# Input projection of a two-block layer: three rolled loops written out, fewer column sums of squares, and a gate product with its weight halves side by side

## The reference, cut to what matters

```
h = rmsnorm(x, norm1_w);  proj = h @ w_in            # 1024 x 3592
q,k,v (3 x 4 heads x 128) = silu(causal_dwconv(proj[:, :1536], conv_qkv_w))
z (4 x 128), b_a (4), a_a (4), then 3 x 512 columns for a second attention
qa = l2norm(qa) * 128**-0.5;  ka = l2norm(ka)        # v is not normalized
beta = sigmoid(b_a);  g = -exp(a_log) * softplus(a_a + dt_bias)
```

## Time and profile before

| | |
|---|---|
| runs, median (lowest to highest) | 2656.86 us (2655.59 to 2659.09) |
| the profiled execution | 2655.63 us |
| its span, first to last instruction | 2654.0 us |
| mean granted TensorE clock | 0.985 |
| busy: PE, PEld, VectorE, ScalarE, GpSimd | 96%, 78%, 57%, 40%, 3% |

### The profile page before, as it was taken

One profiled execution on the slowest core, in us unless ns is written; L12 is line 12 of the kernel. 1 busy time (PEld: TensorE's weight loads), 2 busy tenths in 40 slices (PEclk: granted clock), 3 DMA queues, 4 the chain that ended last, 5 costly groups with the idle time before them and its releaser, 6 DMA issues.

```text
span 2654.0 us, 36131 instructions
## 1 busy us (share of the span) xinstructions
PE 2536.4 (96%) x14218; PEld 2078.6 (78%) x14218; DVE 1506.7 (57%) x2521; ACT 1061.4 (40%) x1715; POOL 67.2 (3%) x118
## 2 busy tenths in 40 slices
PE   6999988999989999999999999979999999999997
PEld 4878866777768788888788888868888788888886
DVE  4114325656536666665648964476588755655555
ACT  3123323544534534444544454443334433423332
POOL 1000000000000000000000000000000000000000
PEclk9999998999999999999999999999999999999999
DMA  5322212111034455556444555522333333333331
GB/s 187 96 80 89 86 67 95 45 36 55 2 119 129 153 184 198 197 197 204 152 134 128 168 173 175 159 72 82 93 88 88 89 107 90 103 114 100 96 96 64
DMA packets 318470, 304.35 MB, mean 115 GB/s; under 512 B 10223, under 2 KB 277860, under 8 KB 318180
## 3 DMA queue, kind: packets, MB, share of 16 engines
q1 hardware_dynamic: 303332, 243.92, 31.4%
q0 software_dynamic: 14976, 58.20, 5.4%
HBM read 244.41 MB, written 57.67 MB: 114 GB/s over the span
## 4 chain that ended last, share of the span: by engine, by line
PE 84%; DVE 8%; ACT 3%; issue 3%; DMA 2%; SPq 0%; POOLq 0%; POOL 0%; DVEq 0%; ACTq 0%
PE PS L2020 13%; PE PS L2021 13%; PE PS L2022 13%; PE PS L1726 11%; PE PS L2037 6%; PE PS L2039 6%; PE PS L2038 6%; PE PS L1967 3%; PE PS L1851 3%; PE PS L1979 1%; PE PS L1837 1%; PE PS L1955 1%; DVE wl L1276 1%; DVE cg L1673 1%; ACT wh L939 1%
## 5 line engine op out<-in xcount | busy, mean ns | idle before, releaser
L2020 PE MATMUL PS<-hh,wh 128*128 128x512 f32 x1728 | 682.7, 395 | 4.3 <-DVE wl L1276 1.9
L2022 PE MATMUL PS<-hh,wl 128*128 128x512 f32 x1728 | 672.9, 389 | 0.0
L2021 PE MATMUL PS<-hl,wh 128*128 128x512 f32 x1728 | 672.5, 389 | 0.0
L939 ACT ACTIVATE wh<-raw 128x1024 fp32r<-128x1024 f32 x352 | 366.7, 1055 | 514.2 <-PE PS L2039 381.1
L1276 DVE TENSOR_TENSOR wl<-raw,wh 128x1024 fp32r<-128x1024 f32 x286 | 347.8, 1227 | 390.2 <-ACT wh L939 389.9
L1569 DVE TENSOR_TENSOR x<-x,PS 128x512 f32<-128x512 f32 x432 | 293.8, 685 | 180.9 <-PE PS L2039 180.1
L2020 PEld LDWEIGHTS PS<-hh,wh 128*128 128x128 f32 x1728 | 324.5, 188 | 76.8 <-issue 5.0
L2021 PEld LDWEIGHTS PS<-hl,wh 128*128 128x128 f32 x1728 | 324.5, 188 | 70.6 <-issue 4.6
L2022 PEld LDWEIGHTS PS<-hh,wl 128*128 128x128 f32 x1728 | 324.3, 188 | 67.8
L2037 PE MATMUL PS<-fh,wh 128*128 128x512 f32 x864 | 344.2, 398 | 18.7 <-DVE x L1569 10.9
L2038 PE MATMUL PS<-fl,wh 128*128 128x512 f32 x864 | 339.4, 393 | 0.0
(11 more groups left out here) (292 smaller groups left out, 2547.8 us busy)
## 6 DMA issues: line engine op xcount, KB each, us to landing
raw<-in_w_ff SPq DMA_DIRECT2D x128, 512.0 KB, 4.0
raw<-in_w_up SPq DMA_DIRECT2D x88, 512.0 KB, 4.4
wl_s<-wl POOLq DMA_DIRECT2D x66, 512.0 KB, 5.4
wl<-wl_s SPq DMA_DIRECT2D x66, 512.0 KB, 3.6
raw<-in_w_in SPq DMA_DIRECT2D x60, 512.0 KB, 4.0
raw<-in_w_down SPq DMA_DIRECT2D x44, 512.0 KB, 5.1
raw<-in_w_out SPq DMA_DIRECT2D x32, 512.0 KB, 3.9
qkvz_s<-st POOLq DMA_DIRECT2D x16, 512.0 KB, 2.9
```

Of the source, the lines that this page charges most:

```text
L939: A(whs(slot), raw[:, k % 2], ACT.Copy).then_inc(s["w_hi"], 1)
L2020: mm(bank, wh[:, k % 4, cut], hh[:, kk, span(a_)], start=kk == 0, stop=False)
L2021: mm(bank, wh[:, k % 4, cut], hl[:, kk, span(a_)], start=False, stop=False)
L2022: last = mm(bank, wl[:, k % 4, cut], hh[:, kk, span(a_)], start=False, stop=kk == KT - 1)
```

## The change

- The five rolled loops over units 12 to 23 are written out, so that each unit can differ.
- The column sums of squares are made for `4*i + u` from 1 to 8 alone, that is for the eight units of q and k. The first square, its semaphore `sq_init` and TensorE's wait for it go. The units of v have no square: their Silu raises `st_written` itself.
- The high and low gate weights lie side by side in one tile `bahl` of 16 columns. One product with `hh` gives high x high and low x high in partitions 0 to 7 and 8 to 15, one with `hl` gives high x low (and low x low, which was not made before). Two products in place of three; the transposes are 16 rows high, and VectorE adds the two halves after them (two more instructions).
- ScalarE waits for `st_written` to reach 24 ahead of the gate copy, and for `st_written` ahead of `cacc` in the last two units of v, in place of the waits that the squares gave.

```diff
-        bah, bal, baw = sb("bah", [P, 8, 8], F32R), sb("bal", [P, 8, 8], F32R), sb("baw", [P, 8, 8])
+        bahl, baw = sb("bahl", [P, 8, 16], F32R), sb("baw", [P, 8, 8])
+        bah, bal = bahl[:, :, 0:8], bahl[:, :, 8:16]
...
# the rolled loops of SyncE, GpSimd's queue, ScalarE, VectorE and TensorE, each:
-            with sp.Fori(0, 3) as i:
+            for i in range(3):
...
# ScalarE
-            act.wait_ge(s["st_written"], 12)
-            A(sqb[:], st[:, 3], ACT.Square).then_inc(s["sq_init"], 1)
...
+                    if i == 2 and u >= 2:
+                        act.wait_ge(s["st_written"], 11 + 4 * i + u)
                     A(cacc[:, u % 2], acc(u % 2), ACT.Copy,
                       scale=par[:, bass.ds(C_CONV + 36 + 4 * i + u, 1)]).then_inc(s["tap0"], 1)
                     act.wait_ge(s["conv"], 12 * i + 3 * u + 3)
                     act.wait_ge(st_free[u], 48 + 16 * i)
-                    A(st[:, u], cacc[:, u % 2], ACT.Silu).then_inc(s["silu"], 1)
-                    act.wait_ge(s["silu"], 4 * i + u + 1)
-
-                    act.wait_ge(s["col_mm"], 4 * i + u + 1)
-                    A(sqb[:], st[:, u], ACT.Square).then_inc(s["st_written"], 1)
+                    if i < 2:
+                        A(st[:, u], cacc[:, u % 2], ACT.Silu).then_inc(s["silu"], 1)
+                        act.wait_ge(s["silu"], 4 * i + u + 1)
+                        if i or u:
+                            act.wait_ge(s["col_mm"], 4 * i + u)
+                        A(sqb[:], st[:, u], ACT.Square).then_inc(s["st_written"], 1)
+                    else:
+                        A(st[:, u], cacc[:, u % 2], ACT.Silu).then_inc(s["st_written"], 1)
             act.wait_ge(s["ba_mm"], 1)
-            A(cacc[0:8, 1, :], acc(2)[0:8], ACT.Copy).then_inc(s["ba_copied"], 1)
+            act.wait_ge(s["st_written"], U_Z)
+            A(cacc[0:16, 1, :], acc(2)[0:16], ACT.Copy).then_inc(s["ba_copied"], 1)
...
# VectorE
-            dve.wait_ge(s["silu"], 12)
-            dve.wait_ge(s["col_mm"], 12)
+            dve.wait_ge(s["st_written"], U_Z)
+            dve.wait_ge(s["col_mm"], 8)
...
-            ba = PS[:, 6, 0:64].rearrange("p (t c) -> p t c", c=8)
+            both = PS[:, 6, 0:128].rearrange("p (t c) -> p t c", c=16)
+            ba = tmpt[:, 7].rearrange("p (t c) -> p t c", c=8)
+            done(V_.tensor_copy(tmpt[:, 6].rearrange("p (t c) -> p t c", c=8), both[:, :, 8:16]))
+            done(TTo(ba, both[:, :, 0:8], tmpt[:, 6].rearrange("p (t c) -> p t c", c=8), ALU.add))
...
# TensorE
-            pe.wait_ge(s["sq_init"], 1)
...
-                    pe.wait_ge(s["st_written"], 12 + 4 * i + u)
-                    for tt in range(TT):
-                        last = mm(PS[:, 7, bass.ds(tt * 12 + 4 * i + u, 1)], sqb[:, tt * P:(tt + 1) * P], ones[:, 0:1],
-                                  start=True, stop=True)
-                    last.then_inc(s["col_mm"], 1)
+                    if 0 < 4 * i + u <= 8:
+                        pe.wait_ge(s["st_written"], 12 + 4 * i + u)
+                        for tt in range(TT):
+                            last = mm(PS[:, 7, bass.ds(tt * 12 + 4 * i + u, 1)], sqb[:, tt * P:(tt + 1) * P], ones[:, 0:1],
+                                      start=True, stop=True)
+                        last.then_inc(s["col_mm"], 1)
...
             for kk in range(KT):
-                for n, (w, h) in enumerate(((bah, hh), (bah, hl), (bal, hh))):
+                for n, h in enumerate((hh, hl)):
                     for q in range(2):
-                        last = mm(PS[0:8, 4 + q, :], w[:, kk, :], h[:, kk, q * HALF:(q + 1) * HALF],
-                                  start=kk == 0 and n == 0, stop=kk == KT - 1 and n == 2)
+                        last = mm(PS[0:16, 4 + q, :], bahl[:, kk, :], h[:, kk, q * HALF:(q + 1) * HALF],
+                                  start=kk == 0 and n == 0, stop=kk == KT - 1 and n == 1)
...
-                        last = tr(PS[:, 6, 8 * t:8 * t + 8], cacc[0:8, 1, t * P:(t + 1) * P], ident[0:8, 0:8])
+                        last = tr(PS[:, 6, 16 * t:16 * t + 16], cacc[0:16, 1, t * P:(t + 1) * P], ident[0:16, 0:16])
```

More of the change, by code:

```diff
@@ L697, in program @@
         names = """const_loaded rows_loaded pack_loaded par_mm par_ready consts_set xt_mm x_written x_spilled w_hi w_lo
-            w_used n_sq n_v n_sd n_diag n_R n_x n_hi n_lo n_lo_odd v_chain tap0 conv silu sq_init
+            w_used n_sq n_v n_sd n_diag n_R n_x n_hi n_lo n_lo_odd v_chain tap0 conv silu
             col_mm ba_loaded ba_hi ba_lo ba_mm ba_copied st_written phase_end tab_dve tab_act tab_mm tables_loaded
@@ L891, in _ @@
                 pool.dma_start(qkvb_s[:, n], st[:, n % 4]).then_inc(st_free[n % 4], 16)
-            with pool.Fori(0, 3) as i:
+            for i in range(3):
                 for u in range(4):
@@ L974, in _ @@
             act.wait_ge(s["ba_loaded"], 16)
-            A(bah[:], baw[:], ACT.Copy).then_inc(s["ba_hi"], 1)
+            A(bah, baw[:], ACT.Copy).then_inc(s["ba_hi"], 1)
             for n in range(12):
@@ L983, in _ @@
                 A(st[:, n % 4], acc(n % 2), ACT.Copy, scale=(0.125 if n < 4 else 1.0)).then_inc(s["st_written"], 1)
-            act.wait_ge(s["st_written"], 12)
-            A(sqb[:], st[:, 3], ACT.Square).then_inc(s["sq_init"], 1)
-            with act.Fori(0, 3) as i:
+            for i in range(3):
                 for u in range(4):
@@ L1343, in _ @@
             dve.wait_ge(s["ba_hi"], 1)
-            TTo(bal[:], baw[:], bah[:].bitcast(F32), ALU.subtract).then_inc(s["ba_lo"], 1)
+            TTo(bal, baw[:], bah.bitcast(F32), ALU.subtract).then_inc(s["ba_lo"], 1)
             for n in range(12):
                 prep(n + 2, (n + 2) % 4)
-            with dve.Fori(0, 3) as i:
+            for i in range(3):
                 for u in range(4):
@@ L1795, in _ @@
                 unit(n, n % 4, n % 2, stats=0 if n == 0 else None)
-            pe.wait_ge(s["sq_init"], 1)
-            with pe.Fori(0, 3) as i:
+            for i in range(3):
                 for u in range(4):
```

## The result

The changed kernel took 2638.14 us (median of 4 runs, 2636.18 to 2639.78) against 2656.23 us for the kernel before beside it; the ratio is 0.9931, 95% interval 0.9914 to 0.9948. It is faster by about 18 us, where 15.2 were forecast, and the median lies 3.6 us under the forecast of 2641.7 us. That is outside the forecast's own range (2639.5 to 2643.5 us) and 0.14 us inside the wide one (2638 to 2646.5 us). The profiled execution took 2636.18 us, with a span of 2634.4 us.

A forecast was written before the change was run, and what follows sets the result against it. TensorE, whose matmuls hold 84% of the span, was taken as the bound. 4.26 + 7.25 + 3.70 = 15.2 us off the 2656.86 us median gave 2641.7 us (ratio 0.9943), own range 2639.5 to 2643.5, wide range 2638 to 2646.5.

The forecast's parts named there:

- Wait and slow start ahead of unit 12: TensorE before unit 12: without the first square's wait, 2.69 us of lateness and 1.57 us of low-clock pairs go, 4.26 us.
- Column sums: TensorE after units 12, 21, 22 and 23: four of twelve sets removed, 3 x 1.85 + 1.70 = 7.25 us.
- Gate product: TensorE after the units of v: sixteen pairs in place of 24, still 0.463 us each, saving 3.70 us.
- "I take 0": Units 12 to 23: writing out the rolled loops gains nothing, bounded by 1.8 us either way.
- The deadlines: ScalarE's and VectorE's marks that TensorE needs in units 12 to 23 and the gate product: all met in time.
- The tightest: Unit 12's finished mark: due at 194.69 us, unit 13 ending at 196.29, slack 1.6 us.
- The two added VectorE instructions: Tables after the gate transposes: both put at 0.45 us with waits, covered by 2.4 us until ScalarE's table load ends.
- keeps its length: Everything behind the stage, its last store and barrier included, starts 15.2 us sooner with unchanged duration.
- Rivals A: At the changed pieces: less gained, through a hidden wait, slower 16-column products or the sums; 11.3 us, 2645.5 us; chance 0.07.
- C: Second stage: low-clock stretches fall otherwise and give part back; half of 8 us lost gives 2645.7 us; chance 0.06.
- D: Units 12 to 23: ScalarE and VectorE become the bound through four table loads a unit; 2664.9 us; chance 0.02.
- Rival B: Units 12 to 23: written-out code gains more than the pieces, as loops slow the queues; 17.2 us, 2639.7 us; chance 0.05.

## Why the prediction was right or wrong

**The stage.** The mechanism was right: each term stood up on its own and in the sum. Wait and slow start ahead of unit 12: 4.26 forecast, 4.24 measured. Column sums: 7.25 and 7.30. Gate product: 3.70 and 3.57, and 11.11 - 7.42 = 3.69 in the changed kernel (317.01 to 324.43 us). Together: 15.2 forecast, 15.18 measured in the first profiles, 15.11 as the sum of the three measured singly. That it is right to 0.02 us is in part luck, as the stage of the kernel before differs by 0.12 us between two profiles.

**"I take 0" for the rolled loops.** Wrong alone, right in the sum. Writing them out saved 1.75 us where TensorE waited ahead of unit 12, as matmuls followed the square 0.33 us sooner and at full clock. Once the wait is gone it saves nothing. The rule from the Trainium skill (Runtime: NRT & Kernel Launch, section Instruction fetch mechanics), that a jump out of the fetched pages stalls, did not show on TensorE: no iteration's edge cost time, and what the loop cost was at its entry. No run tells whether the jump's target was still among the fetched pages, in which case the rule asks for no stall.

**The deadlines.** All were met; TensorE had no wait between the first units and the barrier. The tightest was looser than forecast. Unit 12's finished mark came at 188.95 + 1.06 = 190.01 us, 3.4 us ahead of unit 13's end, not 1.6. Forecast from the rolled loop, Silu's table load stood behind the wait for the convolution (195.51 us, behind the last tap). Written out, it stands ahead of that wait, beside VectorE's taps (timeline of ScalarE; with written-out loops alone it stands there too, at 189.16 us):

```profile
182.76 1.12 ACT L991 ACTIVATE cacc<-PS,par 128x1024 f32<-128x1024 f32 x1 [8.91 <-PE PS L1733]
183.90 1.28 ACT L996 ACT_TABLE_LOAD   x1
```

The two added VectorE instructions took 0.21 and 0.23 us and were covered by ScalarE's table load, as forecast.

**The time.** The step that failed is the last of the sum: 15.2 us taken off a median of three runs, with everything else at 0 because it "keeps its length". That everything outside the stage keeps its length is not so from one execution to the next: in the first pair of profiles it was worth 4.4 us. Two things are in the 3.3 to 3.6 us. First, the reference. Over all 75 runs of the kernel before, its median is 2654.5 us (2651.4 to 2660.2), 2.3 below the median of the three that I built on. Three runs of a kernel that spreads by 8.8 us don't give a base to 1 us, and my range took in only the spread of the three. Second, the difference itself. Over 14 runs of the changed kernel (median 2638.4, 2633.9 to 2640.4) it is 16.1 us by medians (95% of resamples between 14.7 and 18.9) and 17.5 by means (16.3 to 18.7). Against only the 28 runs of the kernel before that were made beside them it is 15.5 (14.1 to 18.3) and 16.9 (15.6 to 18.2). The stage gives 15.2. What lies outside the stage differs between profiles of one kernel by up to 4 us: 2300.0 and 2301.3 us for the kernel before, 2295.6, 2298.9 and 2299.8 for the changed one, and 2296.8 to 2306.1 us for the eight kernels with other edits inside the stage. That the changed kernel finds the short form of these stretches more often is what the means suggest, and three of its profiles (mean 2298.1 us) against ten of the others (2301.2) don't settle it. What difference there is lies behind the second stage, with 1885.7 to 1886.2 us in these three and 1886.3 to 1892.0 in the ten; but with idle work at its start and barrier the changed kernel had 1891.4 us there, so the short form isn't tied to it. This part, 1 to 2 us, stays open. Rivals A, C and D did not come: no piece gained less, the second stage kept its length to 0.03 us in the first pair, and ScalarE has one table load in units 12 to 23. (Rival D's sum is 2664.7 us, not 2664.9, with the rounded 23 us.) Rival B (more is gained through the written-out code) had nearly the right time, 2639.7 us, and the wrong reason: written out alone, the kernel's median didn't fall.

## What to carry to other kernels

Where one engine holds the chain, price an edit by the distance from start to start of its instructions, including how the next one starts, and then check every deadline: here that gave the stage to 0.1 us. Compare two profiles by marks at the edges of the changed part and not by their spans, since the parts that nobody touched differed by more than some of the terms. Add the spread of the untouched parts to the range of the time, and take the reference from many runs. Savings at one wait (its cause removed, its release sooner, the clock behind it) are one saving, not several.

## What the runs showed of the hardware that was not expected

- Matmuls with 16 weight columns are as far apart as with 8: 0.463 us a pair of 512 columns, where 128 columns have 0.453. Their weight load takes 94 ns, between the 88 of 8 columns and the 188 of 128, and doesn't show in the distance.
- TensorE's clock fell behind waits of 2.49 to 2.52 us (five profiles) and 2.85 us (one), and did not behind 1.77, 2.20 (two profiles) and 2.48 us (one).
- The same kernel starts unit 0 at 37.1 or at 40.4 us. Of the 3.3 us, 1.8 are two products that take 1.95 or 3.75 us, and the other 1.5 had come up ahead of them (they start at 31.3 or 32.8 us).
- Work that nobody reads, put into two waits of about 6 us, one of 3 and the load at the start, took the changed kernel from 2638.4 to 2630.4 us. At the start and at a barrier behind which loads are waited for, it gave nothing (2640.6 us).
